# Half of the neighbourhood units turn their probabilities with a DMA transpose; the output weights come in pieces of 256 KB

## The reference, cut to what matters

```python
s_loc = einsum('bwhd,biwjhd->bhwij', qr, kwin) * ATTN_SCALE + bias
s_ctx = einsum('bwhd,bchd->bhwc', qr, kc) * ATTN_SCALE
p = softmax(concatenate([s_loc, s_ctx], -1), axis=-1)
out = einsum(p_loc, vwin) + einsum(p_ctx, vc)
mix = concatenate([hyena, gqa, out], -1) @ w_out
```

## Time and profile before

| | |
|---|---|
| median of 3 runs | 1250.11 us (1246.34 to 1251.19) |
| profiled execution, its own time | 1246.36 us |
| its span | 1244.6 us |
| mean granted TensorE clock | 0.997 of full speed |
| neighbourhood units, first to last maximum | 269.6 to 374.2 us of the span |

### The profile page before, as it was taken

The page is one execution under the profiler, slowest core; times in us unless marked ns, Lnnn a source line. Parts: engine busy times, 40 slices in busy tenths (PEclk is TensorE's granted clock), DMA queues, the critical chain, the costliest instruction groups (busy, mean ns, idle before and its releaser), DMA issues. The chain is left out here.

```text
span 1244.6 us, 22496 instructions
## 1 busy us (share of the span) xinstructions
PE 1222.9 (98%) x7981; PEld 662.6 (53%) x7981; DVE 980.4 (79%) x1597; ACT 642.0 (52%) x1213; POOL 398.0 (32%) x385
## 2 busy tenths in 40 slices
PE   8999999998999999999999999999999999999998
PEld 1564656555765666664455455555555554444444
DVE  3879998675879999964489888888888885666587
ACT  2642234545779999963145554455555543412425
POOL 0000000114678988840320444445554320000001
PEclk9999999999999999999999999999999999999999
DMA  9728723257320130021300332222223317997953
GB/s 353 284 88 319 259 80 136 81 119 157 95 53 19 35 137 20 18 86 51 119 34 2 102 102 87 90 90 65 89 85 101 101 33 263 351 346 243 355 209 136
DMA packets 124931, 167.74 MB, mean 135 GB/s; under 512 B 22449, under 2 KB 83889, under 8 KB 123441
## 3 DMA queue, kind: packets, MB, share of 16 engines
q1 hardware_dynamic: 124848, 166.65, 40.5%
HBM read 138.57 MB, written 22.55 MB: 129 GB/s over the span
## 5 line engine op out<-in xcount | busy, mean ns | idle before, releaser
L1364 PE MATMUL PS<-arena 128*128 128x512 f16 (+9 forms) x7485 | 1186.4, 319 | 14.8 <-DMA arena<-in_w_mod 5.6
L1364 PEld LDWEIGHTS PS<-arena 128*128 128x128 f16 (+3 forms) x7485 | 617.3, 100 | 559.3 <-issue 36.1
L3161 DVE SCALAR_TENSOR_TENSOR arena<-arena 128x512 f16<-128x512 f32 x128 | 112.4, 885 | 30.3 <-ACT arena L2389 29.6
L2389 ACT ACTIVATE arena<-arena 128x512 f16<-128x512 f32 x120 | 75.4, 631 | 102.0 <-PE PS L1364 102.0
L2519 ACT ACTIVATE arena<-arena 128x512 f16<-128x512 f32 x77 | 48.2, 629 | 124.6 <-DVE arena L3382 75.2
L3045 DVE TENSOR_REDUCE arena<-PS 128x1 f32<-128x512 f32 (+1 forms) x160 | 106.7, 680 | 4.5 <-PE PS L1364 4.5
L1358 POOL TENSOR_TENSOR arena<-arena 128x1 f32<-128x1 f32 x8 | 4.7, 598 | 231.3 <-DVE arena L3549 227.5
L2292 ACT ACTIVATE arena<-PS 128x512 f16<-128x512 f32 x125 | 75.1, 601 | 2.6 <-PE PS L1364 1.5
L1208 POOL TENSOR_TENSOR arena<-arena 128x512 f16<-128x512 f32 x64 | 74.0, 1158 | 6.8 <-ACT arena L2297 4.3
L3218 DVE TENSOR_TENSOR arena<-PS,arena 128x256 f32<-128x256 f32 (+1 forms) x100 | 55.2, 553 | 25.4 <-PE PS L1364 25.1
L3397 DVE SCALAR_TENSOR_TENSOR arena<-arena 128x512 f16<-128x512 f32 x77 | 52.5, 687 | 19.5 <-ACT arena L2519 19.5
(11 more groups left out here) (225 smaller groups left out, 1292.8 us busy)
## 6 DMA issues: line engine op xcount, KB each, us to landing
arena<-in_w_ffn_out SPq DMA_DIRECT2D x121, 256.0 KB, 5.2
arena<-in_w_mod SPq DMA_DIRECT2D x23, 1024.0 KB, 7.3
arena<-in_w_ffn_in SPq DMA_DIRECT2D x88, 256.0 KB, 3.0
left_operands<-arena SPq DMA_DIRECT2D x43, 256.0 KB, 2.9
arena<-in_w_in SPq DMA_DIRECT2D x9, 1024.0 KB, 5.8
arena<-left_operands SPq DMA_DIRECT2D x3, 2816.0 KB, 12.9
arena<-lay_bias SPq DMA_DIRECT2D x12, 512.0 KB, 3.9
arena<-in_x SPq DMA_DIRECT2D x2, 2048.0 KB, 14.0
```

The source lines that it names most:

```text
L1364: return pe.matmul(out, lhsT, rhs, start=start, stop=stop, skip_group_check=True)
L2389: act.activation(block_split(p, b)[:, 0], weight_block(p, b, first), ACT.Copy, scale=WS).then_inc(blk_hi, 1)
L3161: dve.scalar_tensor_tensor(dst[:, 1], src, WS, dst[:, 0], ALU.mult, ALU.subtract).then_inc(blk_lo, 1)
```

## The change

Odd units from v = 3 to v = 29 (14 of 32) are marked `by_dma`. For these the five PE transposes are gone. ACT writes the exponentials back into PSUM, then makes the high part of all 640 columns unturned (`hi_p`), DVE makes the low part unturned (`low_p`, one instruction), both into `Phl` in SBUF (128x1280 in 16 bits), and SyncE turns both parts with one DMA transpose into `PT[1]`. `Phl` and `PT[1]` are single buffers for these units. On PE, `weigh(k-2)` of such a unit goes behind the projection, at the end of iteration k; on DVE `low_p(k-1)` goes right behind `maximum(k)`; on ACT `scaled(k-2)` keeps its place. The output weights come in 16 loads of 256 KB, spread over iterations 6 to 9 and 12 to 15 and after the loop, behind the DMA transposes of the same iteration. `turn_qk` is issued at k = 6, 10, ... in place of 7, 11, ...; the buffer `shifts` moves.

```diff
@@ -310,10 +310,19 @@
         self.v, self.par, self.blk, self.j = v, v % 2, v // 8, v % 8
         self.banks = [range(0, 3), range(3, 5)]
         self.scores_at = 1024 * self.par
+        self.by_dma = v % 2 == 1 and 1 < v < HN * NT - 1
     def turned(self, bank):
-        return 2 * self.v + bank + 1
+        return sum(2 for v in range(self.v) if not Unit(v).by_dma) + bank + 1
+
+    def halves(self, bank=0):
+
+        return sum(1 if Unit(v).by_dma else 2 for v in range(self.v)) + bank + 1
+
+    def landed(self):
+
+        return 16 + 16 * (self.v // 2)
     def turned_at(self, bank):
...
@@ -519,7 +528,8 @@
         gc = f32(Z + 87, NT, 2, HD)
         gk = f32(Z + 91, NT, 2, HD)
         Pb = [f32(o, 5, P) for o in (103, 105.5)]
-        PT = [[f16(o, 5, P) for o in parts] for parts in ((28, 29.25), (30.5, 100))]
+        Phl = f16(105.5, 2, 5 * P)
+        PT = [f16(o, 2 * 5, P) for o in (28, 100)]
         nearV = [f16(o, 4, HN, 2, HD) for o in (20, 24, 32, Z + 91)]
         bias = [f32(o, 1024) for o in (4, 8, 36, 40, 44)]
         natok = f32(Z + 34, NT, HN * HD)
...
@@ -890,7 +902,7 @@
         @block.sync
         def _(sp):
-            def load(c, src, shape):
+            def slot_free(c):
                 before = chunk_before(c)
                 if before is not None:
@@ -907,6 +919,9 @@
                         sp.wait_ge(wo_split, n_of_kind(before, "wo"))
                     else:
                         sp.wait_ge(split_lo, n_split(before))
+
+            def load(c, src, shape):
+                slot_free(c)
                 sp.dma_start((raw16 if CHUNKS[c] in ("fwd", "inv") else raw)(c, *shape), src).then_inc(raw_in[chunk_slot(c)], 16)
             sp.dma_start(cols[:, 0:N_COLS], lay["cols"]).then_inc(cols_in, 16)
@@ -1003,18 +1018,37 @@
                 t0 = (16, 40)[n]
                 sp.dma_start(gates[n].rearrange("(t p) -> p t", p=P), mod[:, t0:t0 + 8, 0],
                              allow_slow_non_contiguous=True).then_inc(gates_out, 16)
-            sp.wait_ge(s_max, n_scored(BiasPiece(BIAS_EARLY - 1).units_done - 1))
-            for n in range(2):
-                load(chunk_index("wo", n), w_out[:, 0:4, 512 * n:512 * n + 512], (4, 512))
+            def load_wo(n, k):
+
+                c = chunk_index("wo", n)
+                if k == 0:
+                    slot_free(c)
+                kt, col = 4 * (n // 2) + k, 512 * (n % 2)
+                sp.dma_start(raw(c, 4, 512)[:, k], w_out[:, kt, col:col + 512]).then_inc(raw_in[chunk_slot(c)], 16)
+
             pieces = {BiasPiece(n - BIAS_RING).units_done: n for n in range(BIAS_EARLY + BIAS_RING, 3 * HN)}
-            for v in range(NNA):
-                if v % 4 == 3 and v > 3:
-                    turn_qk(GROUP0[0] + v // 4 - 1)
-                if v in pieces:
-                    load_bias(pieces[v])
+            def turn_p(u):
+                sp.wait_ge(pt_lo, u.halves())
+                sp.wait_ge(o_mm, u.v - 1)
+                sp.dma_start_transpose(PT[1], flat(Phl)).then_inc(pt_in, 16)
+
+            for k in range(NNA):
+                if k in pieces:
+                    load_bias(pieces[k])
+                if k and Unit(k - 1).by_dma:
+                    turn_p(Unit(k - 1))
+                if k % 4 == 2 and k > 2:
+                    turn_qk(GROUP0[0] + k // 4 - 1)
+                if k == 6:
+                    sp.wait_ge(s_max, n_scored(BiasPiece(BIAS_EARLY - 1).units_done - 1))
+                if 6 <= k < 10:
+                    load_wo(0, k - 6)
+                if 12 <= k < 16:
+                    load_wo(1, k - 12)
             turn_qk(NU - 1)
             for n in range(2, 4):
-                load(chunk_index("wo", n), w_out[:, 4:8, 512 * (n % 2):512 * (n % 2) + 512], (4, 512))
+                for k in range(4):
+                    load_wo(n, k)
             sp.wait_ge(o_mm, NNA)
             for i in range(3):
@@ -1659,7 +1693,7 @@
             def copied(u, bank):
-                pe.wait_ge(pt_lo, u.turned(bank))
+                pe.wait_ge(pt_lo, u.halves(0 if u.by_dma else bank))
             def scores(u):
                 q, k = nqT[:, u.blk, u.j * P:u.j * P + P], nkT[:, u.blk]
@@ -1698,7 +1732,10 @@
                     pe.wait_ge(o_rdy, u.v - 1)
-                copied(u, 1)
+                if u.by_dma:
+                    pe.wait_ge(pt_in, u.landed())
+                else:
+                    copied(u, 1)
                 for i in range(5):
                     m = i - 2 * (bias_kind(u.j) % 2)
                     if 0 <= m < 3:
@@ -1706,7 +1743,7 @@
                     else:
                         v = V[:, NT + m % 3, u.blk] if m > 0 else V[:, NT + m + 2, u.blk]
                     for part, vp in ((0, 0), (1, 0), (0, 1)):
-                        ins = mm(PS[:, 6 + u.par, 0:HD], PT[u.par][part][:, i], v[:, vp],
+                        ins = mm(PS[:, 6 + u.par, 0:HD], PT[u.par][:, 5 * part + i], v[:, vp],
                                  i == 0 and part + vp == 0, i == 4 and vp == 1)
                 ins.then_inc(o_mm, 1)
@@ -1830,11 +1867,15 @@
                     chunk(Step(early_chunk(k)))
                 elif early_chunk(k) is None and free_bank(k)[0] is not None:
                     turn_shifts(Step(0))
-                weigh(Unit(k - 2))
-                turn_p(Unit(k - 1))
+                if not Unit(k - 2).by_dma:
+                    weigh(Unit(k - 2))
+                if not Unit(k - 1).by_dma:
+                    turn_p(Unit(k - 1))
                 for i in range(4):
                     if q_unit(k, i - 3) is not None:
                         project_q(q_unit(k, i - 3), i)
+                if Unit(k - 2).by_dma:
+                    weigh(Unit(k - 2))
                 if early_chunk(k) == NKT:
                     chunk(Step(NKT))
             step(Step(0))
@@ -2255,9 +2296,17 @@
             def exponentials(u):
                 act.wait_ge(s_max, n_scored(u.v))
-                act.activation(flat(Pb[u.par]), PSf[:, u.scores_at:u.scores_at + 5 * P], ACT.Exp,
-                               scale=-1.0, bias=nmax[:, u.par:u.par + 1], accum_out=esum[:, u.v % 4:u.v % 4 + 1])\
-                    .then_inc(s_exp, 1)
+                ps = PSf[:, u.scores_at:u.scores_at + 5 * P]
+                if u.v == NNA - 1:
+                    act.wait_ge(pt_in, u.ahead(-2).landed())
+                act.activation(ps if u.by_dma else flat(Pb[u.par]), ps, ACT.Exp, scale=-1.0,
+                               bias=nmax[:, u.par:u.par + 1], accum_out=esum[:, u.v % 4:u.v % 4 + 1]).then_inc(s_exp, 1)
+
+            def hi_p(u):
+                if u.v > 3:
+                    act.wait_ge(pt_in, u.ahead(-2).landed())
+                act.wait_ge(s_exp, u.v + 1)
+                act.activation(Phl[:, 0], PSf[:, u.scores_at:u.scores_at + 5 * P], ACT.Copy, scale=PSC).then_inc(pt_hi, 1)
             def copy_p(u):
                 if u.v >= 2:
@@ -2266,7 +2315,7 @@
                 for b, t in enumerate(u.banks):
                     act.wait_ge(pt_mm, u.turned(b))
                     o = u.turned_at(b)
-                    act.activation(flat(PT[u.par][0][:, t.start:t.stop]), PSf[:, o:o + len(t) * P],
+                    act.activation(flat(PT[u.par][:, t.start:t.stop]), PSf[:, o:o + len(t) * P],
                                    ACT.Copy, scale=PSC).then_inc(pt_hi, 1)
             def scaled(u):
@@ -2327,8 +2376,11 @@
                     from_psum(q_unit(k, 1))
                 if k > 2:
                     scaled(Unit(k - 2))
-                copy_p(Unit(k - 1))
+                if not Unit(k - 1).by_dma:
+                    copy_p(Unit(k - 1))
                 exponentials(Unit(k))
+                if Unit(k).by_dma:
+                    hi_p(Unit(k))
                 if k == 2:
                     act.wait_ge(near_in[0], 16 * 13)
                     scaled(Unit(0))
@@ -3018,11 +3070,16 @@
             def low_p(u):
+                if u.by_dma:
+                    dve.wait_ge(pt_hi, u.halves())
+                    dve.scalar_tensor_tensor(Phl[:, 1], PSf[:, u.scores_at:u.scores_at + 5 * P], PSC, Phl[:, 0],
+                                             ALU.mult, ALU.subtract).then_inc(pt_lo, 1)
+                    return
                 for b, t in enumerate(u.banks):
-                    dve.wait_ge(pt_hi, u.turned(b))
+                    dve.wait_ge(pt_hi, u.halves(b))
                     o = u.turned_at(b)
-                    dve.scalar_tensor_tensor(flat(PT[u.par][1][:, t.start:t.stop]), PSf[:, o:o + len(t) * P], PSC,
-                                             flat(PT[u.par][0][:, t.start:t.stop]), ALU.mult, ALU.subtract)\
+                    dve.scalar_tensor_tensor(flat(PT[u.par][:, 5 + t.start:5 + t.stop]), PSf[:, o:o + len(t) * P], PSC,
+                                             flat(PT[u.par][:, t.start:t.stop]), ALU.mult, ALU.subtract)\
                         .then_inc(pt_lo, 1)
             def inverse_sum(u):
@@ -3106,6 +3163,8 @@
```

(13 more changed lines are left out.)

## The result

The changed kernel takes **1279.1 us** in the median of 6 runs (1277.6 to 1281.4), the kernel before on the same chips 1248.3 us (6 runs): a ratio of **1.025** (95% interval 1.023 to 1.027). The forecast of slower was right, and its 1279 us is met to half a microsecond (its terms add up to 1279.5). Part by part it was less exact: two errors of some 3 us each, of opposite sign, make the agreement that close. The profiled execution took 1278.8 us, its span 1276.9.

The account below looks back on a forecast made before the run. PE was taken to bound the kernel before, a cross-engine two-unit loop the changed one: 293.5 + 13 x 8.5 = 404.0 against 374.61, +29.4 on 1246.4 gives 1275.8, plus 3.7 to the median, 1279 us; range 1264 to 1304.

Parts of the forecast that it names:

- ACT keeps scaled(k-2), copy(k-1), Exp(k): ACT's list for odd k: a late weigh(k-2) holds up unit k's Exp, halves, DMA and weigh, closing a two-unit loop.
- PE idles about 1.7 us in each pair: Before the scores after an odd iteration, PE waits for the low part, about 1.7 us a pair.
- PE at some 65% in stretches between 300 and 390 us: Sign expected in the changed profile if right: PE some 65% busy in the loop's stretches.
- A pair of 8.5 us: Loop over two units in the neighbourhood stage: 8.5 us a pair where it took 6.0, for 13 pairs.
- S+2.36: Forecast start of the maximum of k+1 on DVE, 2.36 us after S, the start of scaled(k-2).
- S+4.12: Forecast issue of the transpose by SyncE, 4.12 us after S, the start of scaled(k-2).
- If it falls once in each pair: Clock rival: PE's idle gaps lower the clock each pair, 1.8 us each, 23 us more, 1302 us; chance 0.17.
- the transpose lands at 292.4; `scaled(3)` starts at 293.5: Start of the loop: unit 3's low part ends at 289.1, its transpose lands at 292.4, scaled(3) starts at 293.5.
- The gain from the pieces: Both PE stalls behind the 1 MB output-weight loads taken as gone: 4.1 + 2.0 = 6.1 us.
- The 3.7 us from profiled execution to median: Median of the runs taken as 3.7 us above the profiled execution, turning 1275.8 into 1279 us.
- The transpose in time: Rival: the DMA transpose lands before PE reaches weigh; a pair takes 7.5 us, median 1266 us; chance 0.08.
- the gain would be 7.0 + 6.1: Rival: no loop closes and PE stays the bound; turns and stalls saved give 13.1 us, 1237 us; chance 0.05.

Follow-up runs that it names:

- e2: Changed kernel with ACT's scaled(k-2) of a DMA-turned unit moved behind the exponentials and high part of unit k: 1253.5 us, ratio 1.005.
- e5: Changed kernel with gate stores behind the loop and scaled(k-2) behind the high part of k: 1247.8 us, ratio 1.001.
- e6: As e5, and on DVE the low part of k goes ahead of the maximum of k+1: 1241.6 us, ratio 0.9965.
- e12: Changed kernel with only DVE's order changed, low part of k ahead of the maximum of k+1: 1275.9 us, ratio 1.023.
- e1: Changed kernel with the two 4 KB gate stores issued behind the loop over the units instead of ahead of it: 1272.0 us, ratio 1.019.
- e7: Kernel before, 1 MB loads kept, with only the gate stores moved behind the loop: 1244.0 us, ratio 0.998.
- e3: Kernel before with output weights in 16 pieces at the changed kernel's places and turn_qk an iteration earlier, all turns on PE: 1241.4 us, ratio 0.995.
- e10: e3 once more, on one chip with e9: 1240.5 us, ratio 0.995.
- e9: e6 with unit 29 turned on PE again, 13 units by DMA: 1240.8 us, ratio 0.996.
- e8: Changed kernel with each 1280-column DMA transpose split into two of 640, the high half sent when made: 1272.4 us, ratio 1.023.

## Why the prediction was right, and where it was not

**The loop closed by ACT's list: right, and shown.** The steps "ACT keeps scaled(k-2), copy(k-1), Exp(k)" and "PE idles about 1.7 us in each pair" stand: PE idles 1.44 us, its weight loads 1.56. e2 takes the order away and with it 25.6 of the 31 us (the low clock in the pairs, some 3 us, goes with it). The sign "PE at some 65% in stretches between 300 and 390 us" was not met: it is 77% in the mean, as the pairs are shorter than forecast.

**A pair of 8.5 us: 7.9, a term too large by several small links.** The maximum starts at S+2.10, not S+2.36, and ends the wait of `low_p` 0.75 us after its start, since the next instruction of DVE runs beside the read-out of the accumulator (both start at 361.17); I had added 0.89. So SyncE issues at S+3.70, not S+4.12. The landing, 3.4 us, is 0.1 above the forecast. From the first weight load of `weigh`, at 365.47, to `scaled` it is 0.73 us; I took 1.04, an interval of before in which another matmul lay between (22 weight loads in the earlier trace rows, where scores and `weigh` have 21). Together -0.6 a pair, 13 times.

**The clock: the rival was partly true.** "If it falls once in each pair" came true in 5 of the 13 (at 327, 344, 368 and 385 us, and through the first, up to 306 us). Seven of the eight other pairs took 7.9 to 8.0 us (one 8.4, as its transpose came half a microsecond later) and the four pairs at low clock 8.6, so such a pair costs 0.7 us and not the 1.8 assumed; with the first, which took 9.17 behind the wait of 7.24 us, that gives back some 4 us. In e2, e5 and e6, where PE's gap for the low part is gone, the clock stays at 1.00 throughout the steady part; but it does so in e12 too, where this gap stands in every pair. So these gaps alone don't bring the clock down, and why it fell in four pairs stays open. It is not the cause of the long pairs: e12 has 7.76 us at full clock. The Trainium skill (TensorE: Matmul & The Clock Gate, HAM oscillation) tells of waits on DMA of 3 to 5 us, longer than any gap inside these pairs, so "by it this case would be likely" read more into it than it says; and its clock is low at the start of every burst, which the trace has in 5 of 13 pairs.

**The step that failed: "the transpose lands at 292.4; `scaled(3)` starts at 293.5".** It started 6.3 us later. I blamed the 1 MB loads for the slow transpose of before and so took the first transpose of the changed kernel, with no large load ahead of it, at its usual time. e1 shows what stands behind it: the stores of the gates, which I had priced nowhere, because the change leaves them alone. It moves a transpose to just behind them. With the stores moved, `scaled(3)` starts at 293.05 (e1), where the forecast had it. e7 takes both stalls of the earlier trace rows away with the 1 MB loads in place, so they were not the loads' alone. The gain from the pieces came to its forecast all the same, 6.1 us forecast, 5.8 and 6.2 measured (e3, e10), since the loads no longer stand in the queue while it is slow. That the medians gain as much as the two stalls together is in part luck: in e7, where both stalls are gone too, they gain 1.8. The Trainium skill (DMA: Bandwidth & Descriptors, Specifications) says that transfers under 512 bytes make the DMA engine read, modify and write. The runs agree that these stores are dear, but the 13 us to their landing and the queue's 38 to 41 GB/s after them come from the trace. The packets of the transposes, 256 bytes, are under 512 too, and with the stores moved they land in 3.3 to 3.5 us (e1), so packets under 512 bytes are not slow by that alone. Whether it is the 4-byte elements, their number (2048) or the mechanism that the skill names, no run tells apart.

**The sum.** +6.3 at the start of the loop and -3.2 in it make the profiled execution 3.0 us longer than the 1275.8 forecast. The 3.7 us from profiled execution to median, taken over from before, were 0.3 here, which cancels it (1275.8 + 3.7 is 1279.5, written as 1279). The close agreement is luck in these two; the range of the main case, 1268 to 1290, is what the method can give.

**The transpose in time, PE as the bound.** No landing under 3.3 us: the first rival is out. The second, "the gain would be 7.0 + 6.1", is out in the changed kernel, and also in the best orders: 6.1 is there, but of the 7.0 only some 1 to 2 us remain in the loop (e6, e9), and none in the median. The chain of an odd unit, Exp, high part, low part, issue and landing, is just about as long as PE's two units (5.6 us a pair where nothing waits, e6), and each transpose that is late, as behind the loads of the same queue, takes back what the turns gave.

**Where the time went**, in order of size: ACT's order 25.6 us (e2), the first transpose behind the gate stores 7.1 us (e1), DVE's order 6.2 us behind the other two (e6 against e5, on one chip) and alone no gain that the medians show (e12), against some 6 us gained by the pieces and their places. What stays open: where the clock falls in those executions of e7 that take 2 to 3 us more, why it falls in some of the loop's pairs and not in others of the same gaps, and whether the size of the loads matters or only their place.

## What to carry to other kernels

Before work goes from TensorE to a DMA, write down the whole loop through every engine's own list: an engine that is half idle can still close it, and here the order of two lines was worth more than three times the work saved. Compare the DMA's latency, issue included, with the slack of that chain and not with the time taken off PE. And look at what is already in the queue ahead of the first such transfer; a few kilobytes in 4-byte elements can cost it 7 us.

## What the runs showed of the hardware that was not expected

- Two stores of 4 KB each in 4-byte elements land 13 us after issue, and from 290 to 298 us, behind them, the queue moves 38 to 41 GB/s, whether the packets are of 256 bytes or of 2 KB.
- A transposing DMA lands after 2.5 us for 512 columns, 2.6 for 640, 3.0 for 1024 and 3.4 for 1280. A straight line through the four, an estimate, has some 1.9 us at no columns and 220 GB/s; the prediction's 260 came from two of them. The Trainium skill (DMA: Bandwidth & Descriptors, Latency and other measured facts) has 261 GB/s for transposes with a non-contiguous middle dimension and 350 to 400 for contiguous ones; the slope here is under both, and far under the second.
- In the changed kernel the clock fell to 0.50 for some 3 us in 4 of the 12 pairs behind the first. All 12 have a gap of 1.44 us for the low part, and most one of 0.5 to 1.3 us for the DMA. In e12, with the same 1.44 us in every pair, it stayed at 1.00 from 310 to 400 us, and one lone gap of 1.96 us left it at 1.00.
- SyncE spends 1.2 to 1.4 us on the issue of a transpose, sometimes 2.0 and more (e6, e8), so that halving the transfer can make the second half late.
